# Convolution one channel group ahead of the recurrence, with its statistics and the first w_out products inside the last group

## The reference

```python
z = rmsnorm(x) @ w_in          # r|k|v|decay,a,gate lora | GLU (2*1024) | merge gates (2*1024)
# branch A: token shift, per-token recurrence on a 64x64 state for each of 16 heads
S = S * d_t + sa x b_t + v_t x k_t;   o_t = S r_t
out_a = (groupnorm(o) + bonus) * g
# branch B: causal depthwise convolution of width 31, then a LayerNorm over all 1024 channels
u = glu_a * sigmoid(glu_b)
c = depthwise_conv(concat(conv_state, u)) + conv_b
out_b = silu(layernorm(c))
merged = sigmoid(gate_a) * out_a + sigmoid(gate_b) * out_b
h = x + merged @ w_out
y = rmsnorm(h + moe(rmsnorm(h)))   # 64 experts, top 8, one shared expert
```

## Time and profile before

| what | before |
|---|---|
| median of 3 runs | 1115.92 us (1115.02 to 1118.81) |
| the profiled execution's own time | 1116.3 us |
| its span | 1114.5 us |
| PE busy | 961.8 us (86% of the span) |
| DVE, ACT, POOL busy | 536.9, 226.5, 349.2 us |
| mean granted TensorE clock | 0.94 of full speed |
| DMA | 295.65 MB, mean 265 GB/s |

### The profile page before, as it was taken

One profiled execution on the slowest core, in us unless ns is written; L12 is line 12 of the kernel. 1 busy time (PEld: TensorE's weight loads), 2 busy tenths in 40 slices (PEclk: granted clock), 3 DMA queues, 4 the chain that ended last, 5 costly groups with the idle time before them and its releaser, 6 DMA issues. The chain is left out here.

```text
span 1114.5 us, 17730 instructions
## 1 busy us (share of the span) xinstructions
PE 961.8 (86%) x7221; PEld 560.4 (50%) x7221; DVE 536.9 (48%) x1021; ACT 226.5 (20%) x469; POOL 349.2 (31%) x396
## 2 busy tenths in 40 slices
PE   5999999999999976598998888987988878789896
PEld 4878777877877774257433333333333323333231
DVE  2158759767875867945531101111112334434685
ACT  3241134125113412221111111111111111111012
POOL 0059609914960992001011101011012323312330
PEclk9999999999999999789999988989989888979999
DMA  8645244344524191654699999999999999999931
GB/s 224 187 127 182 96 131 167 110 131 137 181 96 134 61 345 35 246 234 162 262 367 416 418 417 412 412 406 402 403 398 408 400 392 364 403 415 402 390 99 40
DMA packets 98971, 295.65 MB, mean 265 GB/s; under 512 B 19602, under 2 KB 50900, under 8 KB 82231
## 3 DMA queue, kind: packets, MB, share of 16 engines
q1 hardware_dynamic: 80695, 254.02, 60.1%
q0 software_dynamic: 18192, 40.46, 9.7%
HBM read 284.12 MB, written 36.30 MB: 288 GB/s over the span
## 5 line engine op out<-in xcount | busy, mean ns | idle before, releaser
L1278 PE MATMUL bank<-big 64*64 64x64 f32 (+7 forms) x6778 | 905.7, 364 | 129.0 <-DMA big<-in_w_up 72.4
L1278 PEld LDWEIGHTS bank<-big 64*64 64x64 f32 (+3 forms) x6778 | 512.4, 150 | 473.9 <-issue 384.5
L1569 ACT ACTIVATE big<-bank 128x256 f32<-128x256 f32 (+6 forms) x284 | 121.7, 450 | 715.4 <-PE bank L1278 398.9
L1075 POOL DMA_INDIRECT big<-xg,big x32 | 32.4, 1012 | 405.5 <-PE bank L561 354.1
L919 DVE TENSOR_TENSOR big<-big,bank 128x256 f32<-128x256 f32 x32 | 13.5, 420 | 239.5 <-ACT big L1569 239.5
L2039 POOL TENSOR_SCALAR big<-big 128x256 f32<-128x256 f32 x120 | 126.8, 1057 | 1.7
L2051 POOL TENSOR_TENSOR big<-big 128x256 f32<-128x256 f32 x120 | 86.7, 723 | 0.3
L1835 DVE SCALAR_TENSOR_TENSOR big<-big 128x256 f32<-128x256 f32 x120 | 79.2, 660 | 4.1
L979 DVE SCALAR_TENSOR_TENSOR big<-big 128x1024 f32<-128x1024 f32 (+1 forms) x48 | 61.5, 1280 | 16.4 <-DMA big<-yrows,big 13.1
L1092 POOL DMA_INDIRECT big<-yrows,big x48 | 50.3, 1047 | 50.9 <-DVE big L979 28.5
L1569 ACT ACTIVATE big<-big 128x16 f32<-128x16 f32 (+6 forms) x95 | 42.5, 487 | 57.5 <-DVE big L1790 18.5
(11 more groups left out here) (163 smaller groups left out, 412.0 us busy)
## 6 DMA issues: line engine op xcount, KB each, us to landing
big<-in_w_gate SPq DMA_DIRECT2D x64, 1024.0 KB, 15.5
big<-in_w_up SPq DMA_DIRECT2D x64, 1024.0 KB, 20.4
big<-in_w_down SPq DMA_DIRECT2D x64, 1024.0 KB
big<-in_w_in SPq DMA_DIRECT2D x29, 1024.0 KB, 5.5
yrows<-big POOLq DMA_DIRECT2D x32, 512.0 KB, 3.7
big<-in_w_out SPq DMA_DIRECT2D x2, 2048.0 KB, 16.7
big<-in_state_wkv SPq DMA_DIRECT2D x32, 64.0 KB, 2.3
out_wkv_s<-big SPq DMA_DIRECT2D x32, 64.0 KB, 4.0
```

Of the source, the lines that this page charges most:

```text
L1075: pool.indirect_dma_start(out=x[0:n, :], out_offset=None, in_=xg, in_offset=bass.IndirectOffsetOnAxis(ap=idxu[0:n, col:col + 1], axis=0), ...
L1278: return nc.tensor.matmul(out_, lhsT=lhsT, rhs=rhs, start=start, stop=stop)
L1569: return nc.scalar.activation(out_, in_, f, **kw)
```

## The change

The z tiles get a new order, written out in a list. Tiles 6 to 9 of group g+2 stand where those of group g+1 stood, and those of groups 0 and 1 are done before group 0. DVE and POOL convolve group g+1 during group g; group 0's convolution is done before group 0, and the last group has none. u has two buffers. The transposes of the convolution's state move from level 4 to level 1. In the last group, tile 13 goes ahead of the products A, the sums of tiles k = 0 to 5 stand where tile 13 stood, those of 6 and 7 in level 4 (after `sample_conv` in level 2), and the variance goes behind chunk 0's state update with Ln and Exp on ACT in place of Sqrt and the reciprocal. `normal(0..3)` and `merge(0..2)` stand in the four chunks, and six of the w_out product pairs (k = 0 to 2) among chunks 2 and 3 and the group norm's sums.

```diff
-            for n in range(2, 12):
+            for n in range(2, 16):
                 z_tile(n)
+        ORDER = [('lora', 0), ('lora', 1)] + section(0, 6, 10) + section(0, 0, 6) + section(1, 6, 10)
+        for g in range(NG):
+            ORDER += section(g, 10, 14)
+            if g + 1 < NG:
+                ORDER += section(g + 1, 0, 6)
+            if g + 2 < NG:
+                ORDER += section(g + 2, 6, 10)
...
             def rkv_of_next(g, step):
-                if g + 1 == NG and 2 <= step < 14 and step % 2 == 0:
-                    conv_sums(step // 2 - 1)
+                if g + 1 == NG and step in (10, 11, 14, 15):
+                    k, t = step // 4 - 2, step % 2
+                    pe.wait_ge(S['wout_in'], 32)
+                    pe.wait_ge(S['merged_ready'], k + 1)
+                    prompt_out(k, t)
...
-                z_tile(z0 + 13)
+                if g + 1 < NG:
+                    z_tile(zn(g, 13))
+                else:
+                    for k in range(KT - 2):
+                        conv_sums(k)
...
                 between = [
                     lambda: tr_samples(),
-                    lambda: (pe.wait_ge(S['lmask_ready'], 4 * (g + 1)), tr_units(BP)),
+                    lambda: (pe.wait_ge(S['lmask_ready'], 4 * (g + 1)), tr_conv_state(), tr_units(BP)),
                     lambda: tr_units(KP),
                     lambda: tr_v(),
-                    lambda: (tr_conv_state(), tr_new_conv()),
+                    lambda: (tr_new_conv(), conv_sums_end()),
                 ]
...
+                if g + 1 == NG:
+                    pe.wait_ge(S['merged_ready'], 3)
+                    prompt_out(2, 0)
                 pe.wait_ge(S['gsq_ready'], g + 1)
...
+            glu(0)
+            tap = taps(0)
             for i in range(6):
                 shifted_rkv(0, i)
+                for _ in range(4):
+                    next(tap)
+            for _ in tap:
+                pass
+            glu(1)
...
+                    if g + 1 == NG and c == 0:
+                        conv_statistics()
                     if c == 1:
                         sample_part(1)
                         sample_part(2)
                     elif c != 3:
                         sample_part((0, None, 3)[c])
                     some_taps((2, 1, 4, 3)[c])
+                    if g + 1 == NG:
+                        if c:
+                            merge(c - 1)
+                        normal(c)
...
+            taps(0, 0, CW)
             pool.wait_ge(S['late_in'], 64)
             for g in range(NG):
-                taps(g, 0, 6)
+                if g + 1 < NG:
+                    taps(g + 1, 0, 6)
                 pool.wait_ge(S['plain_ready'], 4 * g + 4)
                 link(gp.tensor_tensor(DG.rearrange("p (a c) n -> p a c n", a=2),
...
-                taps(g, 6, CW, lambda w: fill(g, w))
+                if g + 1 < NG:
+                    taps(g + 1, 6, CW, lambda w: fill(g, w))
+                else:
+                    for w in range(6, CW):
+                        fill(g, w)
```

More of the change, by code:

```diff
@@ L180, in layer_step @@
         IP = F.take(2, NCH, CH)
-        UU = F.take(2, CW - 1 + NCOL)
+        UUS = [F.take(2, CW - 1 + NCOL) for _ in range(2)]
         AR = F.take(NU, 2, CH)
@@ L1781, in _, with glu @@
             shifted(1, 25, LZS[1][:, 0, 1, :])
+            def glu(h):
+                for p in range(2):
+                    n = zn(h, 8 + p)
+                    dve.wait_ge(S['z_free_act'], freed('act', zn(h, 6 + p)))
+                    dve.wait_ge(S['zt_mm'], n + 1)
+                    if p == 0 and h >= 2:
+                        dve.wait_ge(S['tr_free'], 8 * (h - 1))
+                        dve.wait_ge(S['tapm'], (2 * CW - 1) * (h - 1))
+                    link(v.tensor_tensor(UUS[h % 2][:, p, CW - 1:CW - 1 + NCOL], ZP[n % 2][:, 0:NCOL], SB[:, p, :], M),
+                         'z_free_dve')
@@ new lines, in taps @@
+            def taps(h):
+                for w in range(CW):
+                    acc, u = C[:, 2 * h, 0:NP], UUS[h % 2][:, 0, w:w + NP]
+                    cw = CWT[:, 2 * h, w:w + 1]
+                    if w == 0:
+                        note(v.tensor_scalar(acc, u, cw, vcol('conv_b', 2 * h), M, AD), 'tap')
+                    else:
+                        dve.wait_ge(S['tap'], CW * h + w)
+                        note(v.scalar_tensor_tensor(out=acc, in0=u, scalar=cw, in1=acc, op0=M, op1=AD), 'tap')
+                    yield
@@ new lines, in sample_conv @@
+            def sample_conv(g):
+                dve.wait_ge(S['tr_free'], 8 * g + 2)
+                for p in range(2):
+                    link(v.tensor_tensor(SCT, SCB[:, p], CWT[:, 2 * g + p].unsqueeze(1).broadcast_to([128, NS, CW]), M),
+                         chain)
+                    link(v.tensor_reduce(SCR8, SCT, AX.X, AD), chain)
+                    link(v.tensor_scalar(C[:, 2 * g + p, NP + 1:NCOL:2], SCR8, vcol('conv_b', 2 * g + p), None, AD), chain)
+                dve.wait_ge(S['tap'], CW * (g + 1))
+                note(v.memset(zero1, 0.0), 'c_ready')
@@ L1826, in _ @@
                 note(ins, 'norm_in')
[L1827 to L1838 removed]
+                tap = taps(g + 1) if g + 1 < NG else iter(())
                 def some_taps(n):
@@ L1895, in _ @@
                     some_taps(2)
+                    if g + 1 == NG and i == 2:
+                        sample_conv(g)
                     if i < len(LEVELS) - 1:
@@ L1964, in _ @@
                 some_taps(CW)
-                for p in range(2):
-                    link(v.tensor_tensor(SCT, SCB[:, p], CWT[:, 2 * g + p].unsqueeze(1).broadcast_to([128, NS, CW]), M),
-                         chain)
-                    link(v.tensor_reduce(SCR8, SCT, AX.X, AD), chain)
-                    link(v.tensor_scalar(C[:, 2 * g + p, NP + 1:NCOL:2], SCR8, col('conv_b', p), None, AD), chain)
-                dve.wait_ge(S['tap'], CW * (g + 1))
-                note(v.memset(zero1, 0.0), 'c_ready')
+                if g + 1 < NG:
+                    sample_conv(g)
+                else:
+                    merge(3)
+                    normal(4)
```

245 lines of the change are left out of this document (125 added, 120 removed).

## The result

The changed kernel takes 1122.83 us (median of 5 runs, 1121.36 to 1125.21), the kernel before 1115.92: ratio 1.0061, 95% interval 1.0041 to 1.0080. Timed once more with the last experiments (`e9_changed_again`) it was 1.0051 (1.0033 to 1.0068). It is slower, by about 6 us, and the forecast of 1128 is 5 us too high: the measured time lies at the very edge of the stated range (1122 to 1134). The profiled execution took 1123.13 us with a span of 1121.3 (before: 1116.3 and 1114.5).

A forecast was written before the change was run, and what follows sets the result against it. PE was taken to bound the groups and the weight stream the experts, which move with the last w_out product. +23.9 to the first state update, -19.0 behind it, +6.9 for the clock: +11.8, 1128 us, range 1122 to 1134.

The forecast's parts named there:

- "faster" rival: Last group's levels: w_out's load no longer disturbs PE, up to 5 us back; total +6.9, or -5.0 (1111); chance 0.17.
- Steps 1 and 2: Before group 0: four z tiles on PE +14.8, later DVE and ACT start +0.7, wait for POOL's DG +5 us.
- Steps 3 and 4: Transposes in level 1 cost 1.9 us over three groups; from group 2 into group 3, 0.9 us gained.
- Step 5: Group 3's levels and first state update: transposes +0.6, sums +1.3, `sample_conv` +0.9, taps gone -0.4; together +2.4 us (1 to 4).
- The sign that I had named: Last group's first state update was to come near 440 us: 412.9 + 24 + 3.2 for the clock.
- Step 6: Last group's states: DVE loses taps but gains normals, merges and statistics, +3.3 us on 19.9.
- Step 7: Group norm: +3.0 us to `gd_ready`, +0.3 ahead of the variance product, -9.7 to `ma_ready` without the channel statistics.
- Step 8: w_out products behind the group norm: 19.9 us in place of 35.8, so -15.9; pairs already done save PE 10.3.
- Step 9: PE's clock halves after four long idle stretches: +1.5, +1.7, +2.0 and +1.7 us, sum 6.9 (0 to 9).

The follow-up runs named there:

- Experiment 1: Changed kernel, but in group 0 POOL makes DG before the first six taps of group 1, not behind them; ratio 1.0013 to the kernel before.
- Experiment 6: Changed kernel, but z tiles 12 and 13 of group 3 are done between groups 2 and 3, not in front of the levels; ratio 0.9985 to the kernel before.
- kernel 3: Kernel before, but in the last group POOL issues its eight padding-row stores at once ahead of taps 6 to 30; ratio 0.9963 to the kernel before.
- experiment 2: Changed kernel, but the last group's eight padding-row stores are spread over its levels; run twice, ratios 1.0091 and 1.0083 to the kernel before.
- kernel 5: Changed kernel, but no w_out product stands ahead of the group norm's end: k = 0 to 2 follow the variance product; ratio 1.0010 to the kernel before.
- experiment 7: Changed kernel with eight added, unused products of 272 columns in group 3's states to hold the clock; ratio 1.0079 to the kernel before.

## Why the prediction was right, and where not

The direction and the places were right, and most prices too. That the time lies inside the range was luck in part: 1122.8 is 0.8 us above its lower bound (and 0.2 below the 1123 that the chances name), and one term of the sum was 5.5 us off, more than the whole miss. By the prediction's own "faster" rival in its milder form, 11.8 - 4.9 = 6.9, the measured +6.8 of the span would have been met.

**Steps 1 and 2 (tiles, DG).** Forecast 106 + 5 = 111.0 for the first level, measured 111.16. DG was forecast at 109.8 and started at 110.04, and POOL's taps began at 45.93 (45.5). Experiment 1 shows the wait to be DG's, and worth its full length.

**Steps 3 and 4, with their part of the clock.** Forecast +24.7 at group 3's first level, measured +24.4. Experiment 6 shows what PE's idling at that boundary is worth: 8.7 us at the end, 7.9 by the ratios, more than all by which the change is slower. The waits were priced right (3.1 and 4.2 us); that two tiles could have filled them I did not see.

**Step 5 is the one that failed.** I forecast +2.4 for the levels and the first update; measured -3.1. The sign that I had named, the first update near 440, was 434.1. The 5.5 us come apart with kernel 3, which has the levels of before without the disturbance: 22.5 us from its first eviction to its first update, 26.7 in before, 23.6 in the changed kernel. So 4.3 us are the disturbance. That it comes from the stores beside the load of w_out, and not from the load alone, rests on experiment 2; kernel 3 moved both. I had this as the ground of the "faster" rival ("up to 5 us come back"), gave that rival 0.17 and left its 4.9 us out of the sum, holding against it that the load stays where it was. The load does stay (issued 5.6 us behind the first eviction before, 6.6 now); what matters is that nothing is stored beside it, and the rows of the waits had the 4.9 us. The other 1.2: level 0 was DVE's by two taps and lost 1.3, which I missed (I took all levels for 4.0 from the earlier trace rows); transposes +0.6 as forecast; level 2 with `sample_conv` +1.1 (0.9); level 3 +0.4; and the stretch with the last sums +0.4, where I had +1.3 and -0.4.

**Step 6 (states).** Forecast +3.3 and 2.0 for the clock, measured 25.3 for 19.9, +5.3. The sum is right, its split is not shown: the O copy waited 3.0 us behind the first pair (kernel 5 has no such wait), and holding the clock gained nothing in experiment 7.

**Step 7 (group norm).** Forecast +3.0, +0.3 and -9.7; measured +3.4, +0.5 and -9.7.

**Step 8 (w_out).** Forecast -15.9 and 1.7 for the clock, -14.2; measured -13.3. The number held, the reading did not: I called the twelve early products "PE's 10.3 us saved", and without them the end is 3.9 us earlier. The prize was that merges need no longer wait for statistics behind the group norm.

**Step 9 (clock).** It fell at all four places, to 0.50 (2.4 to 1.2 GHz). At DG it cost 1.1 us (experiment 1, forecast 1.5), at the boundary of groups 2 and 3 1.6 (experiment 6, forecast 1.7). Ahead of k = 4 the products ran at 0.50 from 479.2 to about 483.2, which I estimate at half of that, 2.0 (forecast 1.7); in the states it is open (2.0). The last two low stretches (439 to 452 and 476 to 483) are no longer together than the one of the kernel before (441 to 461). The Trainium skill (TensorE: Matmul & The Clock Gate, "What's actually happening") puts the penalty of the ramp under 1% of a typical kernel's span and says not to fit a specific count of slow matmuls. The three places that have a number come to 4.7 us, which is 0.4% of 1122, but most of a change worth 6 us.

Together: 24.4 - 3.1 + 5.3 - 5.8 - 13.3 = +7.5 at the last product, forecast +11.8; the difference is step 5 (-5.5) and small terms of the other sign.

## What to carry to other kernels

Work moved ahead of a recurrence is paid for where the bound engine then runs dry: look at both ends of the move for the stretch that lost its filler, and give it some back. Products put ahead of ones that another engine waits for can cost more than they fill, even on an engine that idles there. When PE idles for nothing a releaser explains, see what is stored beside a large load in that stretch; to bunch the stores ahead of it, which also started the load later, was worth 4 us by an edit of a few lines.

## What the runs showed of the hardware that I had not expected

- With stores of 0.5 MB beside a load of 4 MB PE idled by "issue", 4.0 us in 28, at changing places. Loads alone, at a DMA share of 1.02 to 1.06, brought none; with the stores paced beside it 0.8 and 2.1 us came back, and 3 us of time. The load landed in 11.1 us without them and in 16.4 with them. By which path they reach PE no run shows.
- A wait for a semaphore of POOL can stand in the profile as "issue" (4.05 us, which was DG's).
- POOL and DVE slow each other unequally: 0.67 to 1.5 us for POOL's 272 columns, 1.22 to 1.57 for DVE's 1024. Each loses about the rest of the instruction that the other has under way.
- Where PE set the pace, a drop of the clock to 0.50 cost 1.1 us in one place and 1.6 in another. Through some 20 us of small products beside DVE's chain no run shows what it costs.
